# Context queries of a fused attention and expert kernel: projected in two parts, with five expert steps between; keys and values three steps later

## What is computed

```python
def expert_choice_ffn(h, w_router, w_gate, w_up, w_down):
    cap = EC_K * S // N_EXPERTS                      # 2 * 256 // 16 = 32
    g, idx = lax.top_k(aff.transpose(0, 2, 1), cap)
    def run_expert(args):
        xe = h[b_rows, ie]
        he = jax.nn.silu(xe @ wg) * (xe @ wu)        # 1024 -> 2816
        return (he @ wd) * ge[..., None]             # 2816 -> 1024
```

```python
def _mla_q(h, w_dq, q_norm, w_uq, rows, cols):
    q = (_rms_norm(h @ w_dq, q_norm) @ w_uq).reshape(b, s, MLA_HEADS, MLA_NOPE + MLA_ROPE)
def _mla_kv(h, w_dkv, kv_norm, w_ukv, rows, cols):
    ckv = h @ w_dkv
    kv = (_rms_norm(c_kv, kv_norm) @ w_ukv).reshape(b, s, MLA_HEADS, MLA_NOPE + MLA_V)
    qc = _mla_q(hc, ...); kc, vc = _mla_kv(hc, ...)
    out_c = _block_attention(qc, kc, vc, scale) @ w_o
```

## Time and profile before

| | |
|---|---|
| median of 3 runs | 2381.32 us |
| profiled execution | 2381.53 us |
| its span, first to last instruction | 2379.4 us |
| TensorE matmul busy | 2132.0 us (90%) |
| TensorE weight load busy | 1160.3 us (49%) |
| VectorE busy | 739.6 us (31%) |
| ScalarE busy | 228.8 us (10%) |
| GpSimd busy | 52.5 us (2%) |
| moved by DMA | 796.88 MB, mean 335 GB/s |
| mean granted TensorE clock | 0.98 |

### The profile page before, as it was taken

One profiled execution on the slowest core, in us unless ns is written; L12 is line 12 of the kernel. 1 busy time (PEld: TensorE's weight loads), 2 busy tenths in 40 slices (PEclk: granted clock), 3 DMA queues, 4 the chain that ended last, 5 costly groups with the idle time before them and its releaser, 6 DMA issues.

```text
span 2379.4 us, 30170 instructions
## 1 busy us (share of the span) xinstructions
PE 2132.0 (90%) x12962; PEld 1160.3 (49%) x12962; DVE 739.6 (31%) x1553; ACT 228.8 (10%) x539; POOL 52.5 (2%) x117
## 2 busy tenths in 40 slices
PE   8999898889868888888888887998999999999998
PEld 7544353343325334334324332533669846747953
DVE  1242111211300100101101103111348867576876
ACT  1231110000100000000000000001320000160000
POOL 0000000000000000000000000000000003000000
PEclk9999999999999999999999999999999999999999
DMA  8899999999999999999999999999509566325450
GB/s 321 338 421 396 424 384 424 424 425 422 425 425 422 423 423 421 424 423 422 423 423 422 423 423 424 401 418 366 208 19 287 177 212 221 126 79 160 169 194 36
DMA packets 148099, 796.88 MB, mean 335 GB/s; under 512 B 15523, under 2 KB 63370, under 8 KB 94914
## 3 DMA queue, kind: packets, MB, share of 16 engines
q1 hardware_dynamic: 138504, 783.43, 81.5%
q10 hardware_dynamic: 9466, 11.53, 1.5%
HBM read 792.78 MB, written 7.19 MB: 336 GB/s over the span
## 4 chain that ended last, share of the span: by engine, by line
PE 62%; DMA 32%; DVE 3%; issue 1%; ACT 1%; ACTq 0%; SPq 0%; DVEq 0%
DMA ring<-in_mlp_w 12%; DMA ring<-in_w_down 10%; PE ps L2842 9%; PE ps L305 7%; PE ps L2853 7%; PE ps L338 7%; PE ps L2296 5%; DMA ring<-in_w_gate 5%; PE ps L2328 4%; PE ps L284 3%; PE ps L2487 3%; PE ps L2301 3%; DMA ring<-in_w_up 3%; PE ps L2497 2%; PE ps L2859 2%; PE ps L2349 2%
## 5 line engine op out<-in xcount | busy, mean ns | idle before, releaser
L2296 PE MATMUL ps<-ring,xe 128*32 128x512 f32 x2016 | 285.0, 633 | 79.0 <-DMA ring<-in_w_up 37.6
L2328 PE MATMUL ps<-ring,expert_work 128*32 128x512 f32 x1408 | 248.3, 659 | 47.6 <-DMA ring<-in_w_down 36.4
L2369 DVE SCALAR_TENSOR_TENSOR expert_work<-expert_work,ps 128x512 f32<-128x512 f32 (+1 forms) x32 | 17.6, 549 | 580.0 <-ACT expert_work L2355 580.0
L2301 PE MATMUL ps<-ring,xe 128*32 128x256 f32 x2016 | 196.9, 460 | 0.0
L2328 PEld LDWEIGHTS ps<-ring,expert_work 128*32 128x32 f32 x1408 | 60.1, 116 | 196.1 <-issue 106.8
L2301 PEld LDWEIGHTS ps<-ring,xe 128*32 128x32 f32 x2016 | 68.9, 110 | 164.8 <-issue 164.8
L2296 PEld LDWEIGHTS ps<-ring,xe 128*32 128x32 f32 x2016 | 54.2, 112 | 193.1 <-issue 60.7
L2497 PE MATMUL ps<-ring,c_qT 128*128 128x512 f32 x256 | 114.9, 602 | 11.9 <-DMA ring<-in_mlp_w 11.9
L2487 PE MATMUL ps<-hT,ring 128*128 128x256 f32 x512 | 114.8, 382 | 9.2 <-DMA ring<-in_mlp_w 9.2
L2487 PEld LDWEIGHTS ps<-hT,ring 128*128 128x128 f32 x512 | 96.0, 190 | 31.4 <-DMA ring<-in_mlp_w 15.8
L338 PE MATMUL ps<-hT,ring 128*128 128x256 f32 x384 | 84.1, 380 | 2.0 <-DMA ring<-in_na_w_qkv 1.3
(11 more groups left out here) (572 smaller groups left out, 2644.2 us busy)
## 6 DMA issues: line engine op xcount, KB each, us to landing
ring<-in_w_gate SPq DMA_DIRECT2D x126, 1408.0 KB, 21.9
ring<-in_w_up SPq DMA_DIRECT2D x126, 1408.0 KB, 22.1
ring<-in_w_down SPq DMA_DIRECT2D x112, 1536.0 KB, 23.4
ring<-in_mlp_w SPq DMA_DIRECT2D x96, 1024.0 KB, 8.0
ring<-in_ada_w SPq DMA_DIRECT2D x32, 1536.0 KB, 10.1
ring<-in_na_w_qkv SPq DMA_DIRECT2D x20, 1024.0 KB, 13.5
ring<-in_w_in SPq DMA_DIRECT2D x8, 1536.0 KB, 18.8
ring<-in_w_down SPq DMA_DIRECT2D x16, 512.0 KB, 23.6
```

The costliest lines, as they stand in the source:

```text
L2296: nc.tensor.matmul(ps[32 * j:32 * j + 32, UP if up else GATE, :], xe[:, k, :], w[:, :, 4 * j:4 * j + 4], start=(k == 0), stop=(k == KC - 1))
L2301: last = nc.tensor.matmul(ps[32 * j:32 * j + 32, REST, 256 * up:256 * up + 256], xe[:, k, :], two, start=(k == 0 and not up), stop=(k == K ...
L2328: last = nc.tensor.matmul(ps[32 * j:32 * j + 32, GATE if half else UP, :], hgT[:, at:at + 32], w[:, (c - c0) * D + 512 * half:(c - c0) * D ...
```

## The change

The queries' ten jobs are sent in two calls: jobs 0 to 4 (rotary part and three heads) behind step (1, 3), as all ten were, and jobs 5 to 9 (five heads) behind step (1, 8). Keys and values move from behind step (1, 10) to behind step (1, 13), on TensorE and in the order of the ring. The two `uq` pieces stay where they are in the ring. All jobs, matmuls, loads and bytes stay the same.

```diff
-        CTX_AFTER = {(0, 8): ("dq",), (0, 12): ("dkv",), (1, 3): ("uq",), (1, 10): ("ukv",),
+        CTX_AFTER = {(0, 8): ("dq",), (0, 12): ("dkv",), (1, 3): ("uq",), (1, 13): ("ukv",),
...
                 elif at == (1, 3):
-                    lat.pe_q(pe)
-                elif at == (1, 10):
+                    lat.pe_q(pe, hi=5)
+                elif at == (1, 8):
+                    lat.pe_q(pe, lo=5)
+                elif at == (1, 13):
                     lat.pe_kv(pe)
```

## The result

The changed kernel takes 2389.43 us (median of 6 runs, 2386.65 to 2390.58) against 2380.53 us for the kernel before beside it (6 runs). The ratio is 1.0036, with a 95% interval from 1.0026 to 1.0045: slower by 8.6 us, by an interval of 6.2 to 10.7. The forecast was 2389.0 us and slower.

What follows compares the result with a forecast made beforehand. While the experts run, the ring's bytes at 424 GB/s were taken as the bound. The sum was 2381.53 + 7.6 (five steps) + 0 (keys and values) = 2389.1 us, given as 2389.0, range 2385.3 to 2392.5.

Steps and rivals of the forecast that it cites:

- The bound and the blocked queue: Experts: ring bytes at 424 GB/s set the time; in expert 1, SyncE's wait for job 9 blocks all later loads.
- The term of five steps, 7.6 us: Expert 1's queries: five expert steps of 1.51 us plus 0.1 us switching delay piece 10's issue by 7.6 us.
- The 5.8 us lost before: Expert 1, 308 to 320 us: DMA time already lost in the kernel before, while loads stand still.
- rival "faster": Expert 1: slots of steps 4 to 8 refill during the second part, winning 5.8 us, 2375.7 us; chance 0.03.
- After the refill: Behind step 9: TensorE waits about 4 us for piece 10; a load into the empty ring takes 5.9 us.
- What is late next: Steps 14, 15 and down pieces: TensorE 9 to 11 us later, loads 7.6 later; lag caught up in expert 2.
- Keys and values, 0 us: Their move three steps on costs 0 us: the hold, 16.3 us with slow clock, hides behind loads.
- cover of 21.6 us: Loads queued behind `ukv`: 14, 15 and four down pieces, 21.6 us, against the keys and values' hold.
- the whole hold might run at half rate: Keys and values: by the skill's rule, the hold might run at 1.2 GHz throughout, taking 28 us.
- Absorbed in part: Rival: late experts, 1520 to 1540 us, give back at most 2.0 us of the delay, 2387.0 us; chance 0.09.

Runs made afterwards that it cites:

- other two profiles: The kernel before, unchanged, profiled twice more: single executions of 2375.76 and 2376.14 us.
- shortened heads: The kernel before with heads 3 to 7 of the context's queries computed with one matmul of depth instead of four: ratio 0.9997 (0.9988 to 1.0006).
- cut weights: The changed kernel's steps with query weights cut by heads, each half with its own piece and slot: 2376.9 us, ratio 0.9988 against the kernel before.
- move alone: The kernel before with keys and values moved behind step (1, 13), queries left in one part: ratio 0.9994 (0.9984 to 1.0003).

## Why the prediction was right, point by point

**The bound and the blocked queue.** As read. The time follows the ring's lost time in all runs, and SyncE issues nothing during the wait. The changed kernel's one wait on L305 is 32.6 us, not 34.3: the wait of before had 2.2 us of slow clock in it and this one has none, while the steps took a little longer than I reckoned (both below). The next issue is at 324.85 rather than 322.9: this execution was late already, with the second `uq` piece at 297.33, 3.45 us after the earlier trace rows, and had 2.2 us of slow clock less behind it.

**The term of five steps, 7.6 us.** Right in kind, a little small in size. I made the sum against an execution whose rotary jobs ran at the slow clock (7.61 us), and so found that step 8 would not wait. At full clock the first part ends 2.2 us earlier, TensorE reaches step 8 before its load does and waits 0.22 us; from the first part's end to the second's start it is 315.92 - 307.86 = 8.06 us, not 7.5. From the second `uq` piece to the next issue it is 324.85 - 297.33 = 27.5 us in the changed kernel. In the first profile of before it is 315.33 - 293.88 = 21.5, with 2.2 of slow clock in it; in the second it is 312.70 - 293.44 = 19.3, and the same in the third. So like against like the hold is 8.2 us longer; the pair of profiles alone would have said 6.1. The runs say 7.9 to 8.6. That the forecast of 2389.0 us stands within 0.5 of the measured 2389.43 is partly luck: the sum started from 2381.53, 1.0 above the median of the kernel before beside it, and added 7.6 where the medians say 8.9.

**The 5.8 us lost before.** The one reading that was wrong for the kernel, though right for its trace: in the other two profiles it is 2.6 to 2.8. It did not enter the sum, but it was the price of the rival "faster", and the expectations for the shortened heads and the cut weights went by it; both gains came out smaller.

**After the refill.** TensorE waits 4.63 us behind step 9 (4 were forecast). The first load takes 6.2 us to land, where the earlier trace rows has 5.9:

```profile
ring<-in_w_gate SPq DMA_DIRECT2D x1, 1408.0 KB, 6.2
```

**What is late next.** Partly wrong, at no cost. The prediction has steps 14 and 15 and what follows 9 to 11 us later on TensorE. Step 14 starts at 363.88, where it started at 344.37: 19.5 us later, 16.1 without the 3.45 of this execution. The prediction's own times already gave 15 or more (`ukv` at 345.5 and 14.0 us of matmuls). From 344 to 392 us the DMA engines still move 409 GB/s or more in every 4 us, so no slot came free too late. The lag was caught up in expert 2, as forecast: TensorE's last matmuls of expert 1 come 15.2 us later, those of expert 2 9.8.

**Keys and values, 0 us.** Right, and shown by the move alone. The slow clock was expected in this hold and came, 16.3 us forecast and 16.21 measured; the chain of waits, as the earlier trace rows:

```profile
315.99 8.83 PE ps L305 x40
...
327.54 20.16 DMA ring<-in_mla_w_ukv
347.74 16.21 PE ps L305 x46
```

The chain also shows the change's mark: it now goes from L305 to the load of `ukv` and back, where it ran through TensorE from 293.88 on. The cover of 21.6 us was right, but a hold must be shorter than its cover by some us to cost nothing. This one, 16.2 us under 21.6, costs nothing; the first hold of before at full clock, 19.3 us under 20.4, loses 2.6 to 2.8 us.

The granted clock in this hold is 0.50 from 348 to 352 us and 1.00 from 356 on:

```profile
348.00:352.00 4.00, 4.00 (x10) 3.19 (x11) 0.42 (x1) 0.38 (x1) 0.00 (x0) 0.50 1.03 434
```

The Trainium skill ("TensorE: Matmul & The Clock Gate", section "HAM oscillation") says that matmuls behind waits for DMA between short groups start at half rate, and the trace agrees. That the whole hold might run at half rate, as the prediction has it by that rule, is more than the section says. Here the slow part cost 2.2 us over the 14.0.

**Absorbed in part.** Not so: the late stretch has the same 0.90 share 8 us later (359 GB/s, against 363 of the earlier trace rows), with TensorE busy throughout. It moved as a whole. The last matmuls of the last expert come at 1646.73, where they came at 1636.54: 10.2 us later, 6.7 without the 3.45, where 7 to 8 were forecast against this first profile.

**The spans.** 2388.5 - 2379.4 = 9.1 us. Of these 3.45 were there before the first changed instruction and 6.1 came in expert 1; on balance 0.4 were given back later. The 3.45 are not the change: the second profile of the same changed kernel has the second `uq` piece at 293.12, before, and in the seven other profiles in which the 12 rotary matmuls took 5.42 us it comes between 293.4 and 296.4. What makes one execution later than another there stays open.

## What to carry to other kernels

Where loads are issued in order into a ring, the last reader of a slot decides when everything behind it moves: putting other work between two readers of one piece lengthens its hold by all of that work, even if that work frees other slots. To divide a long step, divide its weights with it, so that each part gives back its own slot. What a hold costs is its length, less the loads queued behind it, plus the restart of the ring (here 2.5 us). By the DMA time lost that sum is still about 1 us short: it gives 1.4 us for the kernel before and 9.6 for the changed one, where the rates show 2.6 to 2.8 and 10.4 to 11.3. And one profiled execution can have the clock of an exception in just that place, so the term that decides is better read in two.

## What the runs showed of the hardware

A restart from an empty ring cost more than I had reckoned: in ten profiles the first piece after the first hold took 5.7 to 6.2 us from issue to landing, where it takes 3.4 us at 424 GB/s. And the granted clock falls in different places in executions of one program: the same 12 matmuls took 7.61 us in one profile of the kernel before and 5.42 in the two others, and the DMA time lost behind them was 5.7 us against 2.6 and 2.8. In one of these two the slow clock was there as well, 4 us earlier, where TensorE had to wait anyway.
